# Spreading sixteen experts' gate rows over partitions: full-height products of single columns, or two transposes and 32-row products side by side

## The reference, cut to what matters

```python
def hierarchical_moe(h, w_rg, b_rg, w_re, b_re, w_e_gate, w_e_up, w_e_down):
    ...
    weight = g_val * e_val
    eid = g_idx * EXPERTS_PER_GROUP + e_idx
    gate = jnp.sum(jax.nn.one_hot(eid, N_EXPERTS, dtype=jnp.float32) * weight[..., None], axis=1)
    act = jax.nn.silu(jnp.einsum('nd,edf->nef', t, w_e_gate)) * jnp.einsum('nd,edf->nef', t, w_e_up)
    act = act * gate[:, :, None].astype(act.dtype)
    out = jnp.einsum('nef,efd->nd', act, w_e_down)
    return out.reshape(bsz, s, d)
```

## Time and profile before

| | us |
|---|---|
| median of three runs | 1421.11 |
| lowest, highest | 1421.02, 1424.01 |
| the profiled execution, its own time | 1422.67 |
| its span, from first to last instruction | 1421.0 |
| TensorE busy in the span | 1370.0 (96%) |
| VectorE busy | 958.3 (67%) |
| ScalarE busy | 629.1 (44%) |
| POOL busy | 78.5 (6%) |
| mean granted clock of TensorE | 0.987 |

### The profile page before, as it was taken

How to read it: one execution, slowest core, us unless ns; L and a number is a source line. 1 busy time by engine, 2 the same in 40 slices (tenths; PEclk the granted TensorE clock), 3 DMA queues, 4 the chain that set the end, 5 groups by cost and what they waited for, 6 DMA issues and landing times.

```text
span 1421.0 us, 25909 instructions
## 1 busy us (share of the span) xinstructions
PE 1370.0 (96%) x10833; PEld 1306.9 (92%) x10833; DVE 958.3 (67%) x1189; ACT 629.1 (44%) x802; POOL 78.5 (6%) x131
## 2 busy tenths in 40 slices
PE   7999999999999999999999998999999987999998
PEld 6999999898899999999888578999999876999998
DVE  5569886654676767677675867888876675645553
ACT  5434435344443333333456634344445444444442
POOL 4013000000000000010100000000000000000000
PEclk9999999999899999999999999999999999999999
DMA  8565535443368887885451045999964421455551
GB/s 238 178 194 178 183 122 177 141 134 124 99 236 280 265 272 258 280 264 185 134 163 60 2 159 187 311 299 317 312 221 149 129 90 31 134 182 187 178 178 60
DMA packets 172579, 259.00 MB, mean 182 GB/s; under 512 B 5125, under 2 KB 147762, under 8 KB 172498
## 3 DMA queue, kind: packets, MB, share of 16 engines
q1 hardware_dynamic: 160890, 203.13, 44.2%
q0 software_dynamic: 10768, 53.43, 11.2%
q10 hardware_dynamic: 840, 1.28, 0.3%
HBM read 256.77 MB, written 1.05 MB: 181 GB/s over the span
## 4 chain that ended last, share of the span: by engine, by line
PE 83%; DVE 10%; ACT 3%; DMA 2%; issue 2%; ACTq 0%; DVEq 0%
PE ring L681 60%; PE acc L681 22%; DVE w_lo L1789 2%; ACT w_hi L1322 2%; DMA raw<-in_w_in_dram 1%; DVE arena L1933 1%; ACT arena L1322 1%; PE acc L1148 1%; PE ring L965 1%; DMA raw<-in_w_mlp_in_dram 1%; DVE arena L1838 0%; DMA raw<-in_w_xo_dram 0%; DVE norm L1804 0%; DMA raw<-in_diff_w_out_dram 0%; DVE stat L2337 0%
## 5 line engine op out<-in xcount | busy, mean ns | idle before, releaser
L1789 DVE TENSOR_TENSOR w_lo<-raw,w_hi 128x2048 fp32r<-128x2048 f32 (+1 forms) x191 | 437.0, 2290 | 302.4 <-ACT w_hi L1322 301.9
L681 PE MATMUL ring<-h_hi,w_hi 128*128 128x256 f32 x2088 | 602.2, 288 | 7.2 <-DVE h_lo L1853 2.6
L681 PE MATMUL ring<-h_lo,w_hi 128*128 128x256 f32 x2088 | 593.8, 284 | 0.0
L681 PE MATMUL ring<-h_hi,w_lo 128*128 128x256 f32 x2088 | 593.7, 284 | 0.0
L1322 ACT ACTIVATE w_hi<-raw 128x2048 fp32r<-128x2048 f32 (+1 forms) x191 | 363.8, 1905 | 248.6 <-DMA raw<-in_w_mlp_out_dram 70.0
L681 PEld LDWEIGHTS ring<-h_hi,w_hi 128*128 128x128 f32 x2088 | 403.4, 193 | 14.2 <-issue 10.5
L681 PEld LDWEIGHTS ring<-h_lo,w_hi 128*128 128x128 f32 x2088 | 403.5, 193 | 2.5 <-issue 2.2
L681 PEld LDWEIGHTS ring<-h_hi,w_lo 128*128 128x128 f32 x2088 | 403.3, 193 | 0.0
L681 PE MATMUL acc<-e_hi,w_hi 128*128 128x256 f32 x768 | 218.8, 285 | 0.1
L681 PE MATMUL acc<-e_lo,w_hi 128*128 128x256 f32 x768 | 217.4, 283 | 0.0
L681 PE MATMUL acc<-e_hi,w_lo 128*128 128x256 f32 x768 | 217.4, 283 | 0.0
(11 more groups left out here) (286 smaller groups left out, 1273.6 us busy)
## 6 DMA issues: line engine op xcount, KB each, us to landing
arena<-in_w_ada_dram POOLq DMA_DIRECT2D x64, 768.0 KB, 6.1
raw<-in_w_mlp_in_dram SPq DMA_DIRECT2D x32, 1024.0 KB, 5.7
raw<-in_w_mlp_out_dram SPq DMA_DIRECT2D x32, 1024.0 KB, 5.1
raw<-in_w_in_dram SPq DMA_DIRECT2D x24, 1024.0 KB, 5.3
raw<-in_w_e_gate_dram SPq DMA_DIRECT2D x16, 1024.0 KB, 5.6
raw<-in_w_e_up_dram SPq DMA_DIRECT2D x16, 1024.0 KB, 6.3
raw<-in_w_e_down_dram SPq DMA_DIRECT2D x16, 1024.0 KB, 6.4
raw<-in_diff_w_in_dram SPq DMA_DIRECT2D x12, 1024.0 KB, 5.2
```

The costliest lines, as they stand in the source:

```text
L681: return nc.tensor.matmul(dst, lhs, rhs, start=start, stop=stop, **kw)
L1789: tt(w_lo[q % SPL][:, 0:n], raw[q % RAW][:, 0:n], w_hi[q % SPL][:, 0:n].bitcast(F32), ALU.subtract)\
```

## The change: what it does

VectorE writes the gates of group g (four experts) into columns 32 g to 32 g + 3 of `gate_cols`, a part of the tile `vec_in` that POOL has cleared. TensorE turns `gate_cols` with two transposes into `acc3`; VectorE copies the result (`norm[:, 0, :]`, gate 4 g + i in row 32 g + i). After two `keep_busy` products TensorE multiplies: for each i, four products, one per group, with the 32 rows of the quarter g, and a new table `spread_gates` as stationary operand, which has ones in row i of each quarter. Experts 0 to 7 go to the four `acc` banks, experts 8 to 15 to the four fills `gate_rows`, of which there are now four. ScalarE empties the `acc` banks (`gates_out`), VectorE the four fills, at the place in its program where it waited for them before, behind the four `ada` pieces. `open_sums` gets a wait for `gates_out`. The table (256 KB) is loaded by POOL ahead of the `ada` pieces, into blocks 48 and 49 of the arena. To stay within the number of semaphores, the pairs `_hi` and `_ready` of five split stages share two, with counts that go on from stage to stage.

```diff
@@ -104,6 +104,10 @@
         s[x::32, x, :] = 1
     c["sum_heads"] = e.reshape(P, 2 * 32)
     c["spread_heads"] = s.reshape(P, 2 * P)
+    s = np.zeros((P, 4, P), np.float32)
+    for x in range(4):
+        s[x::32, x, :] = 1
+    c["spread_gates"] = s.reshape(P, 4 * P)
     cnt = np.stack([1.0 / np.minimum(np.arange(T) + 1, w) for w in WINDOWS]).astype(np.float32)
     c["counts"] = np.broadcast_to(cnt.reshape(1, 4 * T), (P, 4 * T)).copy()
     c["slot_id"] = np.broadcast_to(np.arange(4, dtype=np.float32), (P, 4)).copy()
@@ -112,7 +116,7 @@
 
 CONST = [("ident", P), ("ones", P), ("causal", P), ("rotate", P), ("halves", P), ("cmp_mask", 32),
          ("misc", 8), ("sum_rows", 4 * 32), ("sum_heads", 64), ("slot_id", 4)]
-LATE_CONST = [("spread_rows", 4 * P), ("spread_heads", 2 * P), ("counts", 4 * T)]
+LATE_CONST = [("spread_gates", 4 * P), ("spread_rows", 4 * P), ("spread_heads", 2 * P), ("counts", 4 * T)]
 
 
 N_CONST_DMA = len(CONST) - 2
@@ -240,7 +244,7 @@
                     ("c_x", 2), ("c_c", 2), ("c_b", 2), ("u_pool", 2), ("gates", 12), ("x_k", 4), ("ln_stat", 1), ("x_v", 2), ("lv_stat", 1),
                     ("x_v2", 2), ("c_out", 4), ("a_out", 4), ("pool_out", 4), ("w_o", 4), ("x_stat", 1),
                     ("x_q", 4), ("x_att", 2 * X_HEADS), ("x_o", 4), ("ffn_stat", 1), ("router", 1),
-                    ("moe_head", 1), ("gate_rows", 8), ("moe_up0", 1), ("moe", 45), ("f_stat", 1), ("n_stat", 1), ("n_q", 3), ("n_rot0", 1), ("n_q3", 1), ("n_rot1", 1), ("n_ks", 1), ("n_rot2", 1), ("n_kw", 1),
+                    ("moe_head", 1), ("gate_rows", 4), ("moe_up0", 1), ("moe", 45), ("f_stat", 1), ("n_stat", 1), ("n_q", 3), ("n_rot0", 1), ("n_q3", 1), ("n_rot1", 1), ("n_ks", 1), ("n_rot2", 1), ("n_kw", 1),
                     ("n_rot3", 1), ("n_kc", 1), ("n_rot4", 1), ("n_rot5", 1), ("n_sums", 1), ("n_gate", 1), ("cmp_hid_k", 1),
                     ("n_spread", 2), ("n_gate_t", 1), ("cmp_k", 1), ("n_vc", 1), ("n_vs", 1), ("cmp_hid_v", 1),
                     ("cmp_score", 1), ("cmp_v", 1), ("n_att", 2 * HEADS), ("n_o", 4), ("m0_stat", 1), ("mlp0", 2 * CHUNKS - 1),
@@ -270,9 +274,13 @@
         NORMS = ("x", "ffn", "f", "n", "m0", "d", "m1")
         PER_NORM = {"squared": 4, "summed": 1, "scaled": KB, "hi": KB, "ready": KB}
 
+        SPLITS = ("mem", "merged", "xo", "no", "so")
+
         def shared(name):
 
             tag, _, what = name.partition("_")
+            if tag in SPLITS and what in ("hi", "ready"):
+                return "split_" + what, 4 * SPLITS.index(tag)
             if tag not in NORMS or what not in PER_NORM:
                 return name, 0
             before = [t for t in NORMS[:NORMS.index(tag)] if not (t == "f" and what in ("scaled", "hi", "ready"))
@@ -360,7 +368,11 @@
         u_pad = sb("u_pad", [P, 4, T + 16])
         VALS = 24
         SQX, Q, X_P, X_PT = 40, 48, 0, 4
-        ADA, GATE_ROWS, F_GAIN2, HID_T, ADA_RAW = 0, 24, 24, 40, 54
+        ADA, GATE_ROWS, F_GAIN2, HID_T, GATE_SPREAD, ADA_RAW = 0, 24, 24, 40, 48, 54
+        gate_cols = vec_in[:, 1:3, :]
+
+        def gate_bank(i):
+            return acc[i][:] if i < 4 else bank(FL["gate_rows"] + i - 4)
 
         def x_v_fill(i):
             return FL["x_v"] + i if i < 2 else FL["x_v2"] + i - 2
@@ -611,6 +623,9 @@
                 src = (two, four)[g % 2][:, g, 16:W]
                 last = nc.gpsimd.tensor_tensor(u_pad[:, g, 16:W], src, u_pad[:, g, 16:W], ALU.subtract)
             last.then_inc(S("p_done"), 1)
+            pool.wait_ge(S("vecs_turned"), 1)
+            nc.gpsimd.memset(gate_cols, 0.0).then_inc(S("pads"), 1)
+
             def ada_load(turn, l, n, src):
 
                 g = 32 * l + n
@@ -639,7 +654,8 @@
                     ada_load(turn, l, n, at(n))
 
 
-            pool.wait_ge(S("xo_ready"), 4)
+            pool.wait_ge(*sig("xo_ready", 4))
+            pool.dma_start(flat(GATE_SPREAD, 0, 4 * P), a["k_spread_gates"]).then_inc(S("gate_table_landed"), 16)
             ada_loads(0)
 
             fg = vec[:, 0, VEC["f_g"]:VEC["f_g"] + KB]
@@ -918,15 +934,22 @@
             last.then_inc(S("routed"), 1)
             linear_first([PN["moe"]], moe_fill(0), block_ready("ffn_ready"))
             pe.wait_ge(S("gates_made"), 1)
-            for e in range(EXPERTS):
-                f = FL["gate_rows"] + e // 2
-                if e % 2 == 0:
-                    open_fill(f)
-                for t in range(2):
-                    last = mm(bank(f)[:, (e % 2) * T + t * P:(e % 2) * T + (t + 1) * P],
-                              route[:, t, 80 + e:81 + e].to_broadcast([P, P]), ident[:], True, True)
-                if e % 2:
-                    last.then_inc(S("gates_spread"), 1)
+            for t in range(2):
+                last = nc.tensor.transpose(acc[3][:, t * P:(t + 1) * P], gate_cols[:, t, :], ident[:])
+            last.then_inc(S("gates_turned"), 1)
+            keep_busy(FL["gate_rows"], 2)
+            pe.wait_ge(S("gate_table_landed"), 16)
+            pe.wait_ge(S("gates_laid"), 1)
+            for i in range(4):
+                open_fill(FL["gate_rows"] + i)
+            for i in range(4):
+                for g in range(E_GROUPS):
+                    e = 4 * g + i
+                    last = mm(gate_bank(e // 2)[:, (e % 2) * T:(e % 2 + 1) * T], flat(GATE_SPREAD, i * P, P)[32 * g:32 * g + 32],
+                              norm[32 * g:32 * g + 32, 0, :], True, True)
+                    if i == 1:
+                        last.then_inc(S("gates_spread"), 1)
+            last.then_inc(S("gates_spread"), 1)
             linear(PN["moe"] + 1, up_fill(0), KB, 2, lambda k: h_hi[:, k, :], lambda k: h_lo[:, k, :])
 
             def open_sums():
@@ -974,6 +997,7 @@
                 pe.wait_ge(S("act_split"), turn.at("step", e + 1))
                 down(p + 2, e % 2)
 
+            pe.wait_ge(S("gates_out"), 4)
             open_sums()
             with pe.Fori(0, LOOP_TRIPS) as r:
                 turn.reg, turn.step = r, {"panel": 12, "bank": 3, "step": LOOP_STEPS, "piece": 2 * LOOP_STEPS}
@@ -1523,10 +1547,9 @@
 
             expert_silu(0, PN["moe"])
             ahead(PN["moe"] + 1)
-            for i in range(8):
-                f = FL["gate_rows"] + i
-                act.wait_ge(S("gates_spread"), i + 1)
-                func(flat(GATE_ROWS, i * 512, 512), bank(f)[:], ACT.Copy).then_inc(S(f"drained{f % BANKS}"), 1)
+            act.wait_ge(S("gates_spread"), 5)
+            for i in range(4):
+                func(flat(GATE_ROWS, i * 512, 512), acc[i][:], ACT.Copy).then_inc(S("gates_out"), 1)
             ahead(PN["moe"] + 2)
             expert_hi(0)
             act.wait_ge(S("small_landed"), 16 * N_SMALL_DMA)
@@ -2117,9 +2140,12 @@
             step(tt(hot_1, hot_1, hot_2, ALU.add))
             step(tt(hot_1, hot_1, ex, ALU.mult))
             step(tt(hot_1, hot_1, over4(R(67, 1)), ALU.mult))
+            dve.wait_ge(S("pads"), 7)
             for g in range(E_GROUPS):
-                last = tt(R(80 + 4 * g, 4), hot_1, over4(hot_g[:, :, g:g + 1]), ALU.mult)
+                last = tt(gate_cols[:, :, 32 * g:32 * g + 4], hot_1, over4(hot_g[:, :, g:g + 1]), ALU.mult)
             last.then_inc(S("gates_made"), 1)
+            dve.wait_ge(S("gates_turned"), 1)
+            nc.vector.tensor_copy(norm[:, 0, :], acc[3][:, 0:T]).then_inc(S("gates_laid"), 1)
 
             hid = lambda i: flat(HID_T, i * 512, 512)
 
@@ -2189,8 +2215,13 @@
             dve.wait_ge(S("cond_made"), 1)
             for n in range(ADA_FIRST):
                 ada(0, n)
-            for i in range(4, 8):
+            dve.wait_ge(S("gates_spread"), 5)
+            for i in range(4):
+                f = FL["gate_rows"] + i
+                drains(nc.vector.tensor_copy(flat(GATE_ROWS, (i + 4) * 512, 512), bank(f)[:]), f)
+            for i in range(4):
                 drained_wait(dve, FL["gate_rows"] + i)
+            dve.wait_ge(S("gates_out"), 4)
             ahead(PN["moe"] + 2)
             expert_act(0, PN["moe"] + 1)
             expert_lo(0)
```

More of the change, by code:

```diff
@@ L669, in _ @@
                 nc.gpsimd.tensor_copy(pad[:, 0:32:2], vec[:, 2, pe0:pe0 + 16]).then_inc(S("cmp_pads"), 1)
-            pool.wait_ge(S("no_ready"), 4)
+            pool.wait_ge(*sig("no_ready", 4))
             pool.wait_ge(S("mod_turned"), TURNS)
@@ L1166, in n_values @@
                 if br == 0 and b % 2 == 0 and g >= 2:
-                    pe.wait_ge(S("no_ready"), g - 1)
+                    pe.wait_ge(*sig("no_ready", g - 1))
                 pe.wait_ge(S("n_pt_even"), u + 1)
@@ L1987, in merged_low @@
             def merged_low(j):
-                dve.wait_ge(S("merged_hi"), j + 1)
+                dve.wait_ge(*sig("merged_hi", j + 1))
                 s = slice(2 * j, 2 * j + 2)
@@ L2045, in x_o_lo @@
             def x_o_lo(h):
-                dve.wait_ge(S("xo_hi"), h + 1)
+                dve.wait_ge(*sig("xo_hi", h + 1))
                 tt(h_lo[:, 2 * h:2 * h + 2, :].rearrange("p b t -> p (b t)"), acc[h][:],
```

(2 more changed lines are left out.)

## The result

The changed kernel takes 1434.33 us (median of 9 runs), the kernel before, run beside it, 1422.15 us (median of 9). The ratio is 1.0076, with a 95% interval of 1.0057 to 1.0095: slower by 0.8%. One of the nine runs took 1664.28 us at a mean granted clock of 0.745; it stands in the median of nine and not in the ratio. The medians of nine differ by 12.2 us; without that run the median of the changed kernel is 1433.03 us, and the difference 10.9 us, as the ratio has it (0.76% of 1422.15 is 10.8). By the ratio's interval the difference is between 8.1 and 13.5 us. The forecast was +12.0 us.

What follows compares the result with a forecast made beforehand. TensorE's own sequence was taken as the bound (busy 1370.0 of 1421.0 us). A wait of +10.6 and a clock term of +1.4 made +12.0 us on the median of 1421.11: 1433.1 us, range 1430 to 1437.

Steps and rivals of the forecast that it cites:

- (a) to (c): From 389.17 on TensorE: 7.06 us of spreading removed, 3.1 added, ending at 392.3; wait for `gates_laid` covered by `keep_busy`.
- (d): Table's DMA ahead of the `ada` loads on POOL's queue: delay hidden, taken as nothing, +2.0 us kept for the range.
- (e): Before expert 0's up product TensorE waits for VectorE's first copy behind `ada` pieces: start 406.85 instead of 396.23, +10.6 us.
- side by side pays: Rival: both engines empty the banks once products are in, TensorE on at 393.4, -2.8 us, 1418.3 us; chance 0.03.
- (f): After the idle time TensorE's up product restarts at 1.2 GHz: +1.4 us, ends 0 and 2.3.
- (g): Behind the up product: expert 0's split activations come about 7 us after it, wanted some 12.5 after; nothing new late.
- the loop gives it back: Rival: panel supply paces the expert loop, so TensorE catches up at most 5.8 us: +6.2, 1427.3 us; chance 0.06.
- the clock stays down: Rival: all 48 up products at 0.20 us each, 9.6 instead of 5.8 us: +14.4, 1435.5 us; chance 0.08.

## Why the prediction was right, point by point

**(a) to (c), the series on TensorE: right.** It ends at 392.3 (389.12 and 3.1 us); the 16 products take 2.0 us; VectorE's copy for `gates_laid` is done at 389.96, under the `keep_busy` products that start at 389.34.

**(d) the table's DMA: right.** No cost is seen: pieces 0 and 1 start at 393.96 and 395.09 without a wait, as in the earlier trace rows, and TensorE waits for no panel up to 690.

**(e) the moved emptying: right**, and the main term. The up product starts at 406.93 (forecast 406.85), after 14.62 us idle (14.5). The order is what matters: with the copies ahead of the pieces, and nothing else changed, the loss is gone. The rule that decided against the rival *side by side pays* holds here: the Trainium skill, "TensorE: Matmul & The Clock Gate", section "Architectural detail: the array is 16× 32×32, not 1× 128×128", says that VectorE takes its queue strictly in order, and this trace agrees, with 5.54 us of idle time in front of copies that were ready to run. The Trainium skill, "TensorEngine Tiling (Array Packing)", section "PSUM Bottleneck", advises emptying with both engines; here both do so in the changed kernel, and ScalarE alone, with the ring first, comes to `open_sums` 16.4 us sooner than that, and as soon as both engines do with VectorE's copies first (9.97 and 10.01 us). The page's sentence is on how much is emptied at once; here it mattered when the first bank was.

**(f) the clock: right in mechanism, too small.** The step is the term of +1.4 us with ends of 0 and 2.3; it measured 2.7, above its upper end. I had taken the row in which 18 products run in 3.40 us, since it was a dense series that restarts behind idle time. The other row was the nearer one: at 0.50 a product cost 5.60 / 28 = 0.20 us there and 5.90 / 28 = 0.21 here. What made the loss was how long the low clock lasted (5.9 us), and both rows were shorter. I also misread that other row as one behind little work: in the trace of the kernel before TensorE is busy for 5.91 of the 7.00 us from 374 to 381, with small products of the router (128x20) at a mean clock of 0.68. So it never showed what an idle time costs. With TensorE kept busy the clock term is gone.

**(g) nothing new is late: right.** The activations of expert 0 are split at 422.8, 7.2 us behind the up product (forecast about 7), and TensorE wants them at 428.3; it waits for nothing up to 690.

**The sum.** +10.7 and +2.7 make the 13.4 seen locally, 1.4 above the forecast of +12.0. The whole time came out on the other side, +10.9 without the run of 1664.28 us, and the profiled execution at 1431.74 us, 3.0 below the 1434.7 that I had forecast for it. The ratio leaves 8.1 to 13.5 open, so the whole times confirm neither size of the clock term, and that the median of nine (+12.2) lies so near the forecast is partly luck. The rival *the loop gives it back* fell (+13.4 before and behind the loop); *the clock stays down* came true in part only, since it asked for all 48 products at the low level and got 28. *Side by side pays* was right in its arithmetic for another kernel: it said -2.8 us, and the kernels whose first copy follows the products at once gained 2.9 to 3.0 up to `open_sums` (4.1 where it started before the last product).

## What to carry to other kernels

A faster series that fills all banks at once moves the bound to the first bank that must be empty again. Look up, in the program of the engine that empties it, what stands ahead of that copy, above all anything that waits for a DMA; its busy share doesn't tell. Give the copy to an engine that is idle then, let it wait only for its own bank, and count what moves back behind it. Price an idle time of TensorE above its own length: here, in one profile each, 2.4 us of it cost 1.5 us of clock besides, 14.6 us cost 2.7.

## What the runs showed of the hardware that was not expected

- What the clock costs grows far less than the idle time ahead of it: the up product of 5.92 us lost nothing behind 0.81 and 0.91 us, 1.5 us behind 2.37, 2.3 behind 5.34 and 2.7 behind 14.62, and a down product of 5.76 us lost 1.6 behind 2.61. Each is one execution, so how much these vary is open.
- Products of 32 rows by 256 columns in full precision take 0.43 us each where two follow one another in the same quarter of the array, as long as products of 128 rows (0.44); side by side in four quarters 0.125 (2.0 / 16). With the quarters one after another the series of 16 took 4.8 us and not 7.1, since products overlap around each change of quarter.
- Stretches of lower granted clock far behind the change differ between profiled executions by up to 3 us each, in kernels with and without the change, so that two spans differ by 9.0 us where the change cost 13.4.
